# Finished MLP down blocks copied out by ScalarE and added by accumulating transfers, and two more wide chunks in each group

## What is computed

```
for l in range(DEPTH):                      # 2
    h = rmsnorm(x, norm_mix[l])
    ...                                     # projections, attention A and B, gates
    x = x + merged @ w_out[l]
    h = rmsnorm(x, norm_mlp[l])
    x = x + jnp.square(jax.nn.relu(h @ w_up[l])) @ w_down[l]     # 2048 -> 8192 -> 2048
return rmsnorm(x, final_norm)
```

## Time and profile before

| | |
|---|---|
| median of 3 runs | 2672.49 us (2672.11 to 2678.21) |
| the profiled execution | 2673.84 us, of which its span is 2672.1 us |
| busy: PE, DVE, ACT, POOL | 99%, 77%, 54%, 5% of the span |
| granted TensorE clock, mean | 0.999 of full |
| read from HBM, written | 535.15 MB, 38.04 MB |
| DMA, mean | 215 GB/s |

### The profile page before, as it was taken

How to read it: one execution, slowest core, us unless ns; L and a number is a source line. 1 busy time by engine, 2 the same in 40 slices (tenths; PEclk the granted TensorE clock), 3 DMA queues, 4 the chain that set the end, 5 groups by cost and what they waited for, 6 DMA issues and landing times.

```text
span 2672.1 us, 37287 instructions
## 1 busy us (share of the span) xinstructions
PE 2657.7 (99%) x13576; PEld 2232.1 (84%) x13576; DVE 2058.7 (77%) x3051; ACT 1445.5 (54%) x1863; POOL 127.6 (5%) x218
## 2 busy tenths in 40 slices
PE   9999999999999999999999999999999999999998
PEld 7788778888888888888888887788888888888887
DVE  5676568977898897987756755689678988989875
ACT  5545555545565555645445455555456556556554
POOL 0100000000100100100010000000001001000000
PEclk9999999999999999999999999999999999999999
DMA  7885545676775766766687655466677767667574
GB/s 259 235 238 169 178 162 187 225 238 236 236 232 194 238 219 208 240 205 236 227 234 227 219 175 172 161 200 225 228 252 234 229 205 239 209 218 233 190 248 152
DMA packets 179961, 575.56 MB, mean 215 GB/s; under 512 B 23016, under 2 KB 43028, under 8 KB 179664
## 3 DMA queue, kind: packets, MB, share of 16 engines
q1 hardware_dynamic: 166256, 536.94, 61.3%
q0 software_dynamic: 13008, 35.98, 5.1%
q10 hardware_dynamic: 528, 0.37, 0.1%
HBM read 535.15 MB, written 38.04 MB: 215 GB/s over the span
## 4 chain that ended last, share of the span: by engine, by line
PE 92%; DVE 4%; DMA 2%; ACT 1%; issue 1%; SPq 0%; POOLq 0%; POOL 0%; ACTq 0%
PE acc L527 24%; PE acc L529 23%; PE acc L528 23%; PE att L495 2%; PE att L497 2%; PE att L496 2%; PE acc L495 2%; PE acc L497 2%; PE acc L496 2%; PE acc L544 1%; PE acc L543 1%; PE acc L545 1%; DVE w_lo L1311 1%; DMA raw<-in_w_main 1%; DVE w_lo L1332 1%; PE turn L496 1%
## 5 line engine op out<-in xcount | busy, mean ns | idle before, releaser
L1311 DVE TENSOR_TENSOR w_lo<-raw,w_hi 128x1024 fp32r<-128x1024 f32 (+1 forms) x778 | 934.8, 1212 | 410.9 <-ACT w_hi L886 409.0
L886 ACT ACTIVATE w_hi<-raw 128x1024 fp32r<-128x1024 f32 (+1 forms) x778 | 813.4, 1051 | 655.8 <-PE acc L529 485.9
L527 PE MATMUL acc<-w_hi,h_hl 128*128 128x512 f32 x1848 | 736.2, 398 | 0.4 <-DVE w_lo L1311 0.3
L529 PE MATMUL acc<-w_hi,h_hl 128*128 128x512 f32 x1848 | 729.0, 394 | 0.0
L528 PE MATMUL acc<-w_lo,h_hl 128*128 128x512 f32 x1848 | 728.5, 394 | 0.0
L527 PEld LDWEIGHTS acc<-w_hi,h_hl 128*128 128x128 f32 x1848 | 347.9, 188 | 82.7 <-issue 4.6
L529 PEld LDWEIGHTS acc<-w_hi,h_hl 128*128 128x128 f32 x1848 | 347.9, 188 | 81.3
L528 PEld LDWEIGHTS acc<-w_lo,h_hl 128*128 128x128 f32 x1848 | 348.3, 188 | 76.0
L1332 DVE TENSOR_TENSOR w_lo<-raw,w_hi 128x1792 fp32r<-128x1792 f32 x166 | 335.5, 2021 | 38.7 <-ACT w_hi L895 37.8
L527 PE MATMUL acc<-w_hi,o_hl 128*128 128x512 f32 x912 | 360.9, 396 | 0.0
L528 PE MATMUL acc<-w_lo,o_hl 128*128 128x512 f32 x912 | 359.9, 395 | 0.0
(11 more groups left out here) (298 smaller groups left out, 3504.7 us busy)
## 6 DMA issues: line engine op xcount, KB each, us to landing
raw<-in_w_main SPq DMA_DIRECT2D x928, 512.0 KB, 4.2
scratch<-spread SPq DMA_DIRECT2D x37, 512.0 KB, 2.7
moved<-scratch SPq DMA_DIRECT2D x148, 128.0 KB, 3.2
scratch<-spread POOLq DMA_DIRECT2D x30, 512.0 KB, 3.6
moved<-scratch POOLq DMA_DIRECT2D x120, 128.0 KB, 4.9
raw<-in_w_misc SPq DMA_DIRECT2D x16, 336.0 KB, 4.4
bias_b<-bias_rows POOLq DMA_DIRECT2D x32, 96.0 KB, 5.7
xs<-in_x SPq DMA_DIRECT2D x4, 512.0 KB, 7.2
```

The lines of the kernel that those rows point to most:

```text
L527: nc.tensor.matmul(o, a_hi, hi[:, kk], start=(k == 0), stop=False)
L529: last = nc.tensor.matmul(o, a_lo, hi[:, kk], start=False, stop=fin)
L886: nc.scalar.activation(w_hi[s][:, 0:2 * width], raw[r][:, 0:2 * width], ACT.Copy).then_inc(hi_ready, 1)
L1311: nc.vector.tensor_tensor(w_lo[s][:, 0:2 * width], raw[r][:, 0:2 * width], w_hi[s][:, 0:2 * width].bitcast(F32), ALU.subtract).then_inc(lo ...
```

## The change

1. The two banks of a unit are one PSUM tensor of 128 x 2 x 512 (`acc_pair`, `wide_pair`), so that what were two instructions of 128x512 becomes one of 128x1024: the transposes of `spread_block`, the blends of the branches (`take_branch_a`, `take_branch_b`), the adds to x, the last add of `add_up_sides`.
2. `take_down` moves from DVE to ACT. ACT copies the side banks to `stage` and the result banks to `down_main` (the space of `spread`), and POOL adds them by two accumulating transfers of 512 KB: `stage` onto `rest[:, n]`, and `down_main` onto the block of `xs`. ACT waits for the transfers of the block before (`down_added`) ahead of its copies; PE waits for ACT's copies (`down_out`). The transfers of a group's last block are waited for by `take_side(g, 1)` on ACT and `spread_u(g, 1)` on DVE in the next "up 2".
3. Unit "up 1" of the loop gets wide chunks 1 and 3, with the side banks att 2 and turn. Its end is now `take_side` and `take_summed` on ACT and `add_up_sides` on DVE, all inside the next "up 2". `u_moved` of block 0 moves from "up 2" to the end of "up 1".
4. The order inside the units of the last group shifts by a chunk in places, and the three passes are written out on SP, ACT and DVE.

```diff
-WIDE_UP = ((1, 3, 5), (), (1, 3, 5, 7), ())
+WIDE_UP = ((1, 3, 5), (1, 3), (1, 3, 5, 7), ())
+SIDES_OF_UP = (0, 1, 0)
...
+            def add_down(l, g, n):
+
+                pool.wait_ge(down_out, downs_before(l, g, n) + 1)
+                pool.dma_start(rest[:, n], stage[:], accum_op=ALU.add).then_inc(down_added, 16)
+                pool.dma_start(xs[:, :, n * NB:(n + 1) * NB], down_main, accum_op=ALU.add).then_inc(down_added, 16)
...
-                for n in range(POOL_MOVES):
+                pass_on(l, E_U)
+                for g in range(GROUPS - 1):
+                    for n in range(NBLK):
+                        pass_on(l, E_U + g * NBLK + n + 1)
+                    for n in range(NBLK):
+                        add_down(l, g, n)
+                for n in range((GROUPS - 1) * NBLK + 1, POOL_MOVES):
                     pass_on(l, E_U + n)
...
                 def take_side(g, n, end):
                     unit_done(end)
+                    if n == 1:
+                        act.wait_ge(down_added, downs_before(l, g, 0) * 32)
...
+                def take_down(g, n, end):
+
+                    unit_done(end)
+                    if n == 0:
+                        act.wait_ge(spread_ready, l * MOVES + E_U + (g + 1) * NBLK + 1)
+                        act.wait_ge(pool_stored, (l * POOL_MOVES + (g + 1) * NBLK + 1) * 16)
+                    else:
+                        act.wait_ge(down_added, downs_before(l, g, n) * 32)
+                    nc.scalar.activation(stage[:], wide_pair[1 - n % 2], ACT.Copy)
+                    nc.scalar.activation(down_main, acc_pair[1 - n % 2], ACT.Copy).then_inc(down_out, 1)
...
+                        run(g * 64 + (C_MLP + 16), {3: lambda: take_side(g, 1, end + 16), 6: lambda: take_summed(g, 1, sides_count(g, -1))},
+                            {0: lambda: u_sums_hi(g, 0)}, WIDE_UP[2], steps_at(g, AT_UP2))
...
-                    for n in range(1, NBLK):
-                        run(g * 64 + (C_MLP + 40 + 8 * n), wide=WIDE[n], steps=steps_at(g, WIDE_AT[n]))
-                    run(g * 64 + (C_MLP + 72))
+                    run(g * 64 + (C_MLP + 48), (), {3: lambda: take_down(g, 0, end + 48)}, WIDE[1], steps_at(g, WIDE_AT[1]))
+                    run(g * 64 + (C_MLP + 56), {7: lambda: take_down(g, 1, end + 56)}, (), WIDE[2], steps_at(g, WIDE_AT[2]))
+                    run(g * 64 + (C_MLP + 64), (), {7: lambda: take_down(g, 2, end + 64)}, WIDE[3], steps_at(g, WIDE_AT[3]))
+                    run(g * 64 + (C_MLP + 72), (), {5: lambda: take_down(g, 3, end + 72), 7: lambda: u_moved(g, 4)},
+                        WIDE_UP[1], steps_at(g, AT_UP1))
...
-                run(C_MLP + 64 * g + 16, {3: lambda: take_up(g, 1, end + 16, 1)}, {2: lambda: u_moved(g, 0)},
-                    WIDE_UP[2], steps_at(g, AT_UP2))
-                run(C_MLP + 64 * g + 24, {3: lambda: take_side(g, 2, end + 24), 4: lambda: take_summed(g, 2, sides_count(g, 0))},
-                    {2: lambda: u_moved(g, 1)})
+                run(C_MLP + 64 * g + 16, {3: lambda: take_side(g, 1, end + 16), 5: lambda: take_summed(g, 1, sides_count(g, -1))},
+                    (), WIDE_UP[2], steps_at(g, AT_UP2))
+                run(C_MLP + 64 * g + 24, {3: lambda: take_side(g, 2, end + 24), 5: lambda: take_summed(g, 2, sides_count(g, 0))},
+                    {3: lambda: u_moved(g, 1)})
...
-                for t in range(TT):
-                    last = nc.vector.transpose(spread[:, :, :, t, :].rearrange("p j k s -> p k j s"),
-                                               src[:, t, :].rearrange("p (k j s) -> p k j s", k=PIECES, j=QUARTERS))
-                last.then_inc(spread_ready, 1)
+                nc.vector.transpose(spread[:].rearrange("p j k t s -> p t k j s"),
+                                    src.rearrange("p t (k j s) -> p t k j s", k=PIECES, j=QUARTERS)).then_inc(spread_ready, 1)
...
+                        run(g * 64 + (C_MLP + 16), (),
+                            {1: lambda: u_sums_lo(g, 0), 3: lambda: add_up_sides(g, 1, NBLK - 1), 6: lambda: spread_u(g, 1)},
+                            WIDE_UP[2], steps_at(g, AT_UP2))
...
-                    run(g * 64 + (C_MLP + 48), (), {3: lambda: take_down(g, 0, end + 48)}, WIDE[1], steps_at(g, WIDE_AT[1]))
-                    run(g * 64 + (C_MLP + 56), {7: lambda: take_down(g, 1, end + 56)}, (), WIDE[2], steps_at(g, WIDE_AT[2]))
-                    run(g * 64 + (C_MLP + 64), (), {7: lambda: take_down(g, 2, end + 64)}, WIDE[3], steps_at(g, WIDE_AT[3]))
-                    run(g * 64 + (C_MLP + 72), (), {5: lambda: take_down(g, 3, end + 72)})
+                    run(g * 64 + (C_MLP + 48), (), (), WIDE[1], steps_at(g, WIDE_AT[1]))
+                    run(g * 64 + (C_MLP + 56), (), (), WIDE[2], steps_at(g, WIDE_AT[2]))
+                    run(g * 64 + (C_MLP + 64), (), (), WIDE[3], steps_at(g, WIDE_AT[3]))
+                    run(g * 64 + (C_MLP + 72), (), {7: lambda: u_moved(g, 4, g < GROUPS - 2)},
+                        WIDE_UP[1], steps_at(g, AT_UP1))
                 g = GROUPS - 1
-                run(C_MLP + 64 * g + 16, (), {2: lambda: u_moved(g, 0, False), 3: lambda: spread_u(g, 1)},
+                run(C_MLP + 64 * g + 16, (), {3: lambda: add_up_sides(g, 1, NBLK - 1), 5: lambda: spread_u(g, 1)},
                     WIDE_UP[2], steps_at(g, AT_UP2))
```

129 lines of the change are left out of this document (69 added, 60 removed).

## The result

The changed kernel takes 2693.8 us (median of 6 runs, 2686.9 to 2696.7); the kernel before, run beside it, takes 2675.9 (6 runs, 2672.1 to 2678.2). The ratio is 1.0069, with a 95% interval of 1.0059 to 1.0080. It is 17.9 us slower, where 2672.0 was forecast and the range ended at 2678.5. The profiled execution of the changed kernel took 2696.7 us, of which 2694.7 are span, so its traces show some 3 us more than the median.

What follows compares the result with a forecast made beforehand. PE's own stream was taken to bound the MLP. From the profiled 2673.8 us, -3.7 (wide chunks), +2.7 (last group), +1.0 (groups 1 and 2) and -0.5 (merges) gave 2673.3, as the runs' median 2672.0; range 2666.8 to 2678.5.

Steps and rivals of the forecast that it cites:

- PE's stream bounds the MLP; a wide chunk saves 0.31 us: MLP: time shrinks only where plain chunks turn wide; 12 new ones in "up 1" at 0.31 give 3.7 us off.
- DVE's offload is worth nothing by itself: MLP loop: freed DVE time gains nothing unless it pays for more wide chunks; DVE some 2 us lighter a pass.
- ACT's copies cost nothing: Down blocks: 8.5 to 11 us of copies a pass on ACT, covered by its running 4 chunks ahead; cost nothing.
- An undisturbed pair takes 9 us: A block's two 512 KB accumulating transfers, one behind the other in POOL's queue: 9 us, between 3.6 and 39.
- rival 2: Pairs take over 15.2 us, ACT stands at block 3's wait, PE's "up 1" comes late: 2701 us or more; chance 0.08.
- Free up to 15.2 us, then its excess six times: Block 2 to block 3: a pair costs nothing up to 15.2 us, beyond that its excess 6 times.
- Loads may land 8.9 us after their issue: Weight loads: needed some 8.9 us after issue, landing after 4.2, so crowding by the transfers costs nothing.
- rival 3: Pairs land in time but crowd weight loads beyond 9 us: slower, 2684 us; chance 0.12.
- "up 2" in groups 1 and 2: Joining "up 1" side sums inside "up 2" fits; only a late load in "up 3" stalls: +1.0 us, bounds 0 and 5.
- The last group, 1.35 us in each layer: Last group's "up 2": DVE's split for chunk 6 ends late, 1.35 us a layer: +2.7 us, bounds 0 and 5.
- Merged instructions, -0.5: Branch B gate units: merged DVE instructions save 0.06 us each, 0.7 at most; 0.5 us off taken.
- What adding costs: Accumulating pairs: 2.0 + 4 x 1.2 = 6.8 us a pair, every source read counted; would also be free.

Runs made afterwards that it cites:

- experiment 8: Changed kernel with "up 1" of groups 1 to 3 plain and the old order of "up 2"; all copies, transfers and waits kept: 2676.5 us, ratio 1.0006.
- experiment 4: Changed kernel with the wide chunks alone: DVE adds the finished down blocks, no ACT copies, no accumulating transfers; 2678.1 us, ratio 1.0005.
- experiment 2: Changed kernel with both accumulating transfers of each pair cut to 64 of 1024 columns, all else kept; 2678.2 us, ratio 1.0013.
- experiment 12: Changed kernel with chunk 3 of every "up 2" plain instead of wide, all transfers and waits kept; 2684.2 us, ratio 1.0037.
- 3: Changed kernel with both transfers of each pair as plain copies of the same bytes, not adding; 2679.1 us, ratio 1.0012.
- 7: Changed kernel with only the side sums added by accumulating transfer; DVE adds each finished block to x; 2678.1 us, ratio 1.0011.
- experiment 5: Wide chunks alone, DVE making the sums, plus two accumulating transfers a pair into an unused table, no other engine waiting in the MLP loop; 2695.7 us, ratio 1.0077.
- 6: Changed kernel with adds cut to 64 columns and each pair held back by a chain of small transfers; 2700.5 us, ratio 1.0100.
- 10: Changed kernel with one more small transfer to an unused place, between the pairs of blocks 1 and 2 of every group; 2691.1 us, ratio 1.0053.
- 1: Changed kernel with 2048 instead of 1024 bytes of memory for the software queue's descriptors; 2699.4 us, ratio 1.0081.

## Why the prediction was wrong, step by step

- **PE's stream bounds the MLP; a wide chunk saves 0.31 us.** Right. In the changed kernel PE starts chunks 1 and 3 of "up 1" so that they last 2.51 and 2.48 us, in all six units. The 3.7 us are in the sum above.
- **DVE's offload is worth nothing by itself.** Right: experiment 8 is level with the kernel before, and experiment 4, without the offload, with experiment 2.
- **ACT's copies cost nothing.** Right: they take 1.01 to 1.03 us each, and experiment 2 has them all.
- **An undisturbed pair takes 9 us.** Near, and low, where the issues follow each other: 9.8 to 10.6 us from the first issue to the last landing for block 3 (its first 9.65 to the last packet, 853.71 to 863.35), 10.7 to 13.1 for blocks 0 and 1. Wrong for block 2, because of the sentence that the two stand behind each other in POOL's queue. The second issue waits until the first transfer is through, 6.4 to 8.6 us, and the pair takes 15.0 to 17.7 us. That meets rival 2's condition (over 15.2 us) in five groups of six, which I had given 0.08; rival 2's time, 2701 or more, was worked out for 20 us a pair. Nothing in the trace of before could show it: POOL's four fetches in the earlier trace rows follow each other without a gap.
- **Free up to 15.2 us, then its excess six times.** Wrong as a rule. ACT stood 28.0 us in six such waits, and PE did not stall in "up 1" at all, save 1.3 and 0.5 us in two units. The excess was taken from the lead (down to 0.06 us at chunk 6 of "up 1" in group 2) and was paid for one unit later.
- **Loads may land 8.9 us after their issue.** Wrong in what it left out. Beside block 2's pair in group 2 of layer 0 the median was 7.3 us and the longest 8.7, under the bound, but I took the reserve of each load by itself. A load at 7.3 uses lead that later chunks share. That is rival 3 (0.12, 2684 us); its figure came from a bound for single loads and was too low.
- **"up 2" in groups 1 and 2.** This is the step that failed. The layout itself was right to 0.02 us: chunk 4 ready at 9.7, wanted at 10.5, "free". The lead measured there is 0.82 us. But the layout assumed that ACT and DVE enter the unit with their full lead of 3.8 us; the transfers, costed at nothing in another paragraph, take up to 4.0 us of lead at chunk 7 of "up 1" and leave 0.92 of the 3.8 at chunk 3 of "up 2". Each paragraph's cover was real, and it was the same cover. The step was put at +1.0 us for groups 1 and 2 (for a late load in "up 3") and measured 11.2 in their four "up 2". Experiment 12 gives 2.6 us of room back and 12.6 us of stall go; in experiment 8 the old "up 2" has the room, and groups 1 and 2 lose nothing. The prediction had no term for the clock either: 3.2 us behind these waits.
- **The last group, 1.35 us in each layer.** Right: 1.42 to 1.46 us in experiments 2, 3, 4 and 7. The gap stands ahead of chunk 6, with DVE's split as its end, as written. In the change itself the two are 5.0 and 2.8, the lost lead included, and 1.55 of low clock in the first.
- **Merged instructions, -0.5.** Of the right size, but not shown. Three gate units of branch B in layer 1 together come out 0.5 to 1.6 us shorter than before in all fourteen profiles with the merges (0.8 in the change's), yet single units differ in both directions, and there is one profile without the merges to compare with.
- **What adding costs.** The estimate from the Trainium skill's DMA: Bandwidth & Descriptors (Anatomy of one DMA), 6.8 us a pair, is below the 9.8 to 13.1 measured where the issues follow each other. The rule from the Trainium skill's Collectives: The Full Stack (The bandwidth ceiling), that an add reads twice, agrees in direction with the packets (328 and 159 ns). The rule from the Trainium skill's DMA: Bandwidth & Descriptors (Issuing engines are not separate DMA queues) that transfers of all issuers interleave on the same 16 engines spoke against the change, and experiment 5 bears it out: 17.6 us for transfers that no other engine waits for. I named it and gave it 0.12.

What is shown: the loss goes when the same transfers copy instead of adding (3), which makes them both lighter and earlier; load (5) and lateness (6) can each cost as much alone; and the room in "up 2" decides how much is lost (8, 12). What stays open: why the second issue waits in one block of every group. One more small transfer ahead of it takes it away (10), the size of the descriptor memory does not (1). Open too is why the clock fell behind two of the waits and not behind others. Nor do the runs say how the 15.6 us of waiting in "up 2" divide between lateness and load, since the two don't add up: 17.6 and 22 us alone, 17.9 together.
